# A two-layer hybrid encoder step on one core: the loop over the layers written out twice, with two splits of the next layer ahead of the last residual

## The reference

```python
for l in range(DEPTH):
    xp, st_p = trunk_layer(xp, pos_p, lw, None)      # 256 prompt tokens
    xs, st_s = trunk_layer(xs, pos_s, lw, past)      # 64 sample tokens, with caches
y_prompt, y_sample = rms_norm(xp, final_norm), rms_norm(xs, final_norm)

def trunk_layer(x, pos, lw, past):
    proj = jnp.einsum('btd,de->bte', rms_norm(x, norm1), w_in)
    # from proj: A sparse attention (indexer, top-k), B band attention, C a state scan with gate
    mix = jnp.concatenate([o_a, o_b, o_c], axis=-1)
    x = x + jnp.einsum('bte,ed->btd', mix, w_out)
    u = jax.nn.relu(jnp.einsum('btd,df->btf', rms_norm(x, norm2), w_up))
    x = x + jnp.einsum('btf,fd->btd', jnp.square(u), w_down)
    return x, states
```

## Time and profile before

| | us |
|---|---|
| median of 3 runs | 3217.57 |
| lowest and highest | 3210.99, 3218.99 |
| the profiled execution | 3219.5 |
| its span | 3217.9 |
| PE busy / DVE busy / ACT busy / POOL busy | 97% / 52% / 36% / 7% |

### The profile page before, as it was taken

One profiled execution on the slowest core, in us unless ns is written; L12 is line 12 of the kernel. 1 busy time (PEld: TensorE's weight loads), 2 busy tenths in 40 slices (PEclk: granted clock), 3 DMA queues, 4 the chain that ended last, 5 costly groups with the idle time before them and its releaser, 6 DMA issues.

```text
span 3217.9 us, 55061 instructions
## 1 busy us (share of the span) xinstructions
PE 3122.9 (97%) x20829; PEld 3064.4 (95%) x20829; DVE 1685.5 (52%) x2135; ACT 1151.0 (36%) x1376; POOL 233.8 (7%) x248
## 2 busy tenths in 40 slices
PE   6999999899999999999989999998999999999998
PEld 6899999799999999999989999987999999999997
DVE  5574467665444444444456745586644444444443
ACT  4333443243333333333323435432433332333333
POOL 5000000040000000000310000001400000000013
PEclk8999999799999999999999999997999999999998
DMA  6444443145455454454434544522554544544542
GB/s 197 140 148 125 142 143 114 59 131 145 149 150 150 150 148 149 148 149 150 150 106 131 155 147 125 155 83 69 145 148 149 149 150 150 149 148 147 149 150 85
DMA packets 233883, 444.64 MB, mean 138 GB/s; under 512 B 23072, under 2 KB 23520, under 8 KB 233424
## 3 DMA queue, kind: packets, MB, share of 16 engines
q1 hardware_dynamic: 228320, 426.37, 44.4%
q0 software_dynamic: 5424, 16.43, 1.7%
HBM read 430.94 MB, written 12.85 MB: 138 GB/s over the span
## 4 chain that ended last, share of the span: by engine, by line
PE 66%; issue 28%; DVE 3%; POOL 1%; DVEq 1%; POOLq 1%; ACT 1%; ACTq 0%
PE G L690 20%; PE G L691 20%; PE G L692 20%; POOL SS L529 1%; PE M L727 1%; PE M L965 1%; PE M L859 1%; PE M L913 1%; PE M L967 1%; DVE raw_parts L1352 0%; PE M L804 0%; PE M L971 0%; PE M L785 0%; PE M L718 0%; DVE TB L1769 0%
## 5 line engine op out<-in xcount | busy, mean ns | idle before, releaser
L1352 DVE TENSOR_TENSOR raw_parts<-raw,whi 128x1024 fp32r<-128x1024 f32 (+1 forms) x816 | 995.1, 1236 | 868.7 <-ACT whi L1086 851.0
L1086 ACT ACTIVATE whi<-raw 128x1024 fp32r<-128x1024 f32 (+1 forms) x816 | 849.6, 1045 | 1411.5 <-PE G L692 1372.6
L690 PE MATMUL G<-X_parts,whi 128*128 128x320 f32 x3840 | 1200.2, 313 | 25.2 <-DVE raw_parts L1352 22.9
L692 PE MATMUL G<-X_parts,raw_parts 128*128 128x320 f32 x3840 | 1188.7, 310 | 0.0
L691 PE MATMUL G<-X_parts,whi 128*128 128x320 f32 x3840 | 1188.6, 310 | 0.0
L690 PE MATMUL G<-U_parts,whi 128*128 128x320 f32 x2560 | 803.1, 314 | 13.3 <-DVE U_parts L1521 13.3
L691 PE MATMUL G<-U_parts,whi 128*128 128x320 f32 x2560 | 797.3, 311 | 0.0
L692 PE MATMUL G<-U_parts,raw_parts 128*128 128x320 f32 x2560 | 796.7, 311 | 0.0
L690 PEld LDWEIGHTS G<-X_parts,whi 128*128 128x128 f32 x3840 | 723.1, 188 | 32.0 <-issue 21.7
L691 PEld LDWEIGHTS G<-X_parts,whi 128*128 128x128 f32 x3840 | 723.2, 188 | 0.4
L692 PEld LDWEIGHTS G<-X_parts,raw_parts 128*128 128x128 f32 x3840 | 722.9, 188 | 0.0
(11 more groups left out here) (268 smaller groups left out, 1348.0 us busy)
## 6 DMA issues: line engine op xcount, KB each, us to landing
raw<-in_w_up SPq DMA_DIRECT2D x256, 512.0 KB, 3.8
raw<-in_w_down SPq DMA_DIRECT2D x256, 512.0 KB, 3.6
raw<-in_w_in SPq DMA_DIRECT2D x224, 512.0 KB, 3.6
raw<-in_w_out SPq DMA_DIRECT2D x64, 512.0 KB, 3.6
U<-in_x_prompt SPq DMA_DIRECT2D x2, 1024.0 KB, 7.5
out_y_prompt<-U SPq DMA_DIRECT2D x8, 256.0 KB, 2.7
bias_ext<-XC POOLq DMA_DIRECT2D x2, 768.0 KB, 5.0
raw<-in_w_in SPq DMA_DIRECT2D x16, 80.0 KB, 2.0
```

The costliest lines, as they stand in the source:

```text
L690: pe.matmul(out, hi, xh, start=(i == 0 and k == 0), stop=False)
L692: mm = pe.matmul(out, lo, xh, start=False, stop=(c == part[1] - 1 and k == KC - 1))
L1086: act.activation(whi[:, c % 4, :, cols], raw[:, c, :, cols], ACT.Copy).then_inc(high_done.sem, 1)
L1352: dve.tensor_tensor(wlo[:, c, :, cols], raw[:, c, :, cols], whi[:, c % 4, :, cols].bitcast(F32), ALU.subtract)\
```

## The change

All five engines' loops over the layers become Python loops, so the program holds the layer's body twice, each with its layer number as a constant; the MLP's inner loops stay loops. DVE then no longer splits chunks 0 and 1 of layer 1 at slots 0 and 1: it does this at the end of layer 0, ahead of the last residual, as at every other unit change. ACT's high parts of layer 1's chunks 0 to 2 are likewise written at the end of layer 0's loop, right behind those of the last unit.

```diff
-        with sp.Fori(0, DEPTH) as l:
+        for l in range(DEPTH):
...
-        with pool.Fori(0, DEPTH) as l:
+        for l in range(DEPTH):
...
-        with pe.Fori(0, DEPTH) as l:
+        for l in range(DEPTH):
...
-        with act.Fori(0, DEPTH) as l:
-            high_parts(l, 0, 0, 3)
+        for l in range(DEPTH):
+            if l == 0:
+                high_parts(l, 0, 0, 3)
...
             for j in range(N_UP):
-                high_parts(l, UNITS - N_UP + j, 3, CHUNKS + 3 if j < N_UP - 1 else CHUNKS)
+                high_parts(l, UNITS - N_UP + j, 3, CHUNKS + 3 if j < N_UP - 1 or l + 1 < DEPTH else CHUNKS)
...
-        with dve.Fori(0, DEPTH) as l:
+        for l in range(DEPTH):
...
             for slot in range(SLOTS_AB + HALF):
                 q, c = slot // CHUNKS, slot % CHUNKS
-                split_chunk(l, q, c)
+                if l == 0 or slot >= 2:
+                    split_chunk(l, q, c)
...
             for j in range(N_UP):
                 q = UNITS - N_UP + j
                 chunks(l, q, 2, CHUNKS)
-                if j < N_UP - 1:
+                if j < N_UP - 1 or l + 1 < DEPTH:
                     next_unit(l, q)
                 add_residual(q + MORE, j, CHUNKS * (q + 1))
                 new_operand(l, j, 4 + j, x_in)
```

## The result

| | us | range, runs |
|---|---|---|
| before | 3214.31 | 3210.99 to 3218.99, 4 |
| after | 3190.48 | 3189.95 to 3192.06, 4 |
| profiled execution before / after | 3219.5 / 3190.2 | span 3217.9 / 3188.4 |

The ratio is 0.9925, with a 95% interval of 0.9913 to 0.9936. The kernel is faster by 24 us. Forecast were a gain of 10.7 us and a time of 3206.9 us, with a range down to 3200.5. The sign was right, but the gain was more than twice the forecast.

What follows compares the result with a forecast made beforehand. TensorE, busy 97% of the span, was taken as the bound, with time to gain only where it idles or runs at the lower clock. Boundary 8.7 plus constants 2.0 gave 10.7 us: 3217.57 to 3206.9 us, range 3200.5 to 3212.5.

Steps and rivals of the forecast that it cites:

- Part 1: Layer boundary: without the jump back, 4.04 us of issue leave DVE's chain between last residual and next layer's first split.
- Part 2: Layer boundary: DVE's two splits of 1.3 us, moved ahead of the last residual, lie in its wait for PE.
- Part 3: Layer boundary: the third chunk's split comes 0.20 us late, between 0 and 0.4, leaving a boundary gain of 8.7 us.
- Part 4: Outside the MLP's inner loops: register operations ahead of waits go; 38 chain pieces of 0.08 us, taken as 2.0 us.
- The rival of the lower clock: Layer 1's scan: 1.2 GHz stretches fall on other matmuls, 4 us either way, 3203 or 3211 us; chance 0.14 each.
- The stall paid all the same: Layer boundary: DVE still stands 4 us between residual and third chunk's split; gain 4.7 us, 3212.9 us; chance 0.10.
- the slower case: MLP inner loops: the jump back over a quarter costs like the layer's, 25 us in all, 3232 us; chance 0.05.

Runs made afterwards that it cites:

- four_registers: The kernel after, with the layer number in a register again on every engine but GpSimd: 3207.02 us, ratio 0.9961 to the kernel before.
- after_again: The kernel after, unaltered, in five more executions: 3191.00 us.
- dve_register: The kernel after, with the layer number in a register again on DVE alone: 3204.41 us.
- splits_behind: The kernel after, with the first splits of the next layer again behind the last residual: 3197.37 us, ratio 0.9935 to the kernel before.
- scan_pad: The kernel after, with one 128x1 write on DVE ahead of each of the scan's 12 waits for the decays: 3193.99 us.
- gate_fill: The kernel after, with 32 more 128x320 matmuls a layer ahead of the first unit that reads U_parts: 3205.28 us.

## Why the prediction was wrong

- **Part 1, the jump goes: right.** The piece of 4 us is gone. The branch was its cause, as the hint alone showed.
- **Part 2, the splits are covered: right.** TensorE has no idle time at the boundary (70.00 us busy in 70.00).
- **Part 3, the third chunk is late: right**, though by 0.11 us and not 0.20. The boundary gave 8.9 us in the profiled pair, where 8.7 were forecast, and 8.8 between the traces of before and `four_registers`. The 11.7 us between the medians of those two hold 4.1 us of a shorter first scan, which no change at the boundary can have caused.
- **Part 4, waits become constants: wrong, and here the prediction failed.** "I take 2.0 us", between 0 and 3.0, measured 16.0 (10.6 to 17.7) between `four_registers` and the kernel after. The count of 38 pieces by 0.08 us was made on the chain of waits, and so was a sum of idle time at a fixed clock. Two things were missed. First, TensorE's idle time fell by 2.1 us a scan (17.0 to 14.9 and 15.0 in `after_again`; 16.4 and 14.8 in the profiled execution of after), where the scan's ten pieces made 0.8. That registers off that chain cost too is likely, though part of the idle time can have gone with the clock. With registers (`dve_register`) the trace has 117 register operations on DVE in the two scans, 54 and 63, of which the chain had shown ten a scan. Second, and larger, the time of the matmuls in a stretch with a mean clock of 0.83 is no constant. They fell by 7.2 or 7.3 us a scan (112.4 to 105.1 and 132.3 to 125.1), and in the profiled pair 6.4 us of a scan's 8.8 went in one place, where the waits had become shorter by 0.35 us together. In the MLP, at a clock of 1.00, nothing came (930.1 and 930.0 us); its inner loops keep their register operations, as the forecast said.
- **The rival of the lower clock** saw the place and not the mechanism. It had the clock fall on other matmuls of the second scan by chance, with either sign and at most 4 us, from the boundary's shift. It was priced apart from part 4, whose consequence it is, and once, where it comes in each layer. "Two scans 1580 us apart came out alike" was read as stability. It also meant that whatever shortens one shortens both. The rival's own test, a second scan's clock more than 0.02 off 0.83, was met: the earlier trace rows has 0.83 twice, and over the same spans of time after has 0.91 twice. Nor were the two scans of before quite alike: cut at the scan's own matmuls they have 0.83 and 0.85.
- **The stall paid all the same, and the slower case: not seen.** PE's longest inner branch takes 208 ns after (209 before), and the MLP's 290 us are as full as in the earlier trace rows.
- **The range** leaned on the spread of before's runs, 8.0 us, as if it were noise around a fixed cost. It may well be a trace of the same sensitivity: the kernel after, with shorter waits, spreads by 2 to 3 us.

What stays open: what sets the clock of a scan besides its waits; how the 16.0 us divide between time that the waits lost directly and time that the clock gave back, since each feeds the other; and why DVE's registers in the scan and elsewhere cost 14 us together and 5.6 and 3.1 alone.

## What to carry to other kernels

Look at the mean granted clock of a stretch before you price a small edit in it. At 1.00 with TensorE full, a step off the path is worth nothing; where the mean is 0.8 to 0.9 and TensorE waits in short pieces, register operations that the sum had at 0.8 us were worth 5 to 9 us a scan here, and three small writes that added 1.3 us of idle time in two scans lengthened them by 7.2. Cut two traces at the same instruction, not at the same time, and set idle and busy time apart: equal matmuls with less busy time are the sign. And ask whether a slow stretch is followed by another engine's chain that ends no sooner, since then a better clock is worth nothing.

## What was not expected of the hardware

- A jump back over a whole layer costs 4.04 us between DVE's branch and its next instruction and 4348 ns on PE; asked for ahead, 0.54 us and 367 ns, worth 7 us of the kernel before (3217.64 to 3210.5). Between the profiled executions half of the gain lies at the boundary (78.9 to 75.2 us) and half in the second scan (149.3 to 145.2).
- A write of 59 ns ahead of each of 12 waits a layer lengthened the kernel by 3.0 to 3.5 us, with 1.4 us of writes in all.
- In `splits_behind` and `scan_pad` the first scan took 120.0 and 120.3 us, as in the kernel after, and the second, whose instructions are those of after's second but for the pads, 3.0 and 3.4 us more than there. In `gate_fill` matmuls added some 25 us ahead of the first scan lengthened that scan by 4.2 us, with the scan's instructions unchanged. Which stretches get 1.2 GHz depends on more than the waits; that it is the moment of arrival is argued, not shown.
